# Two experts' weights in one piece per partition, loaded in two transfers instead of six

## The reference

```python
scores = sigmoid(xt @ w_router)                       # (tokens, 128)
_, idx = top_k(scores + b_router, 8)
gate = sel / sum(sel) * 2.5
for every expert e, for the tokens that chose it:
    h = silu(xb @ w_e1[e]) * (xb @ w_e3[e])           # w_e1, w_e3: (128, 1024, 256)
    out[tok] += (h @ w_e2[e]) * gate                  # w_e2: (128, 256, 1024)
y = layer_norm(alpha * h + shared_expert + out)
```

## Time and profile before

| what | value |
|---|---|
| median of three runs | 2010.45 us |
| the profiled execution: its own time | 2014.95 us |
| its span, first to last instruction | 2013.2 us |
| mean granted TensorE clock | 0.948 of full speed |
| PE busy | 1789.9 us, 89% |
| DVE, ACT, POOL busy | 630.3, 392.0, 362.4 us |
| moved by DMA | 532.04 MB, of it 488.47 MB by q1 and 41.23 MB by q0 |

### The profile page before, as it was taken

The page is one execution under the profiler, slowest core; times in us unless marked ns, Lnnn a source line. Parts: engine busy times, 40 slices in busy tenths (PEclk is TensorE's granted clock), DMA queues, the critical chain, the costliest instruction groups (busy, mean ns, idle before and its releaser), DMA issues. The chain is left out here.

```text
span 2013.2 us, 29270 instructions
## 1 busy us (share of the span) xinstructions
PE 1789.9 (89%) x10614; PEld 1055.3 (52%) x10614; DVE 630.3 (31%) x1516; ACT 392.0 (19%) x918; POOL 362.4 (18%) x529
## 2 busy tenths in 40 slices
PE   7999997889899999999988878888888888888877
PEld 6857776878778885555433333333333333333332
DVE  1387754774304412521111111111111111111127
ACT  0114544433120101311111111111111111111103
POOL 1000001888880000011111111111111111111100
PEclk8999998989999999999998999998989898989988
DMA  3433312001142425379999999999999999999966
GB/s 118 146 138 105 105 32 48 3 7 47 53 158 80 131 71 187 122 284 418 421 420 415 412 416 404 420 407 410 402 410 396 411 398 407 413 410 419 409 265 250
DMA packets 160782, 532.04 MB, mean 264 GB/s; under 512 B 22061, under 2 KB 88927, under 8 KB 110205
## 3 DMA queue, kind: packets, MB, share of 16 engines
q1 hardware_dynamic: 138921, 488.47, 61.5%
q0 software_dynamic: 20640, 41.23, 5.5%
q10 hardware_dynamic: 1148, 1.34, 0.2%
HBM read 522.52 MB, written 41.42 MB: 280 GB/s over the span
## 5 line engine op out<-in xcount | busy, mean ns | idle before, releaser
L1938 PE MATMUL bank<-arena 128*64 128x512 f32 x2048 | 511.2, 657 | 143.1 <-DMA arena<-in_w_e 141.9
L1938 PEld LDWEIGHTS bank<-arena 128*64 128x64 f32 x2048 | 158.5, 151 | 491.2 <-issue 489.7
L1956 PE MATMUL bank<-arena 128*64 128x512 f32 x1024 | 233.9, 599 | 0.0
L2181 DVE TENSOR_TENSOR arena<-bank,arena 128x256 f32<-128x256 f32 x64 | 27.2, 425 | 580.7 <-ACT arena L2026 580.7
L1806 POOL DMA_INDIRECT arena<-h_rows,index x66 | 66.9, 1013 | 774.4 <-DVE index L2055 717.9
L1425 PE MATMUL bank<-arena 128*128 128x276 f32 x768 | 184.7, 400 | 7.3 <-ACT arena L1527 3.1
L1425 PEld LDWEIGHTS bank<-arena 128*128 128x128 f32 x768 | 146.7, 192 | 41.4 <-ACT arena L1527 3.5
L1201 PE MATMUL bank<-arena 64*64 64x64 f32 (+2 forms) x2816 | 126.7, 246 | 26.7 <-DVE arena L1314 14.7
L2026 ACT ACTIVATE arena<-bank 128x256 f32<-128x256 f32 x64 | 24.6, 385 | 606.2 <-PE bank L1938 606.2
L1201 PEld LDWEIGHTS bank<-arena 64*64 64x64 f32 x2816 | 111.9, 141 | 33.4 <-DVE arena L1314 15.7
L1956 PEld LDWEIGHTS bank<-arena 128*64 128x64 f32 x1024 | 67.8, 136 | 110.8 <-issue 109.6
(11 more groups left out here) (333 smaller groups left out, 1844.0 us busy)
## 6 DMA issues: line engine op xcount, KB each, us to landing
arena<-in_w_e SPq DMA_DIRECT2D x384, 1024.0 KB, 14.2
arena<-in_w_in SPq DMA_DIRECT2D x50, 512.0 KB, 4.2
arena<-routed_rows SPq DMA_DIRECT2D x8, 2048.0 KB, 23.3
arena<-in_w_mem_kv SPq DMA_DIRECT2D x4, 1024.0 KB, 5.8
arena<-in_cache_mem_k SPq DMA_DIRECT2D x8, 512.0 KB, 4.6
arena<-in_cache_mem_v SPq DMA_DIRECT2D x8, 512.0 KB, 5.4
arena<-in_w_out SPq DMA_DIRECT2D x2, 2048.0 KB, 12.6
arena<-in_w_s SPq DMA_DIRECT2D x3, 1024.0 KB, 10.4
```

What stands on the lines that cost most here:

```text
L1938: mm = pe.matmul(p_gu[t * S:(t + 1) * S, :], xt[:, v, c, t * S:(t + 1) * S], w13[2 * v + t][:, :, c, :], start=(c == 0), stop=(c == KD - 1))
L1956: mm = pe.matmul(p_y[h][t * S:(t + 1) * S, :], hidT[:, j, t * S:(t + 1) * S], w2[2 * v + t][:, j, h * 512:(h + 1) * 512], start=(j == 0), ...
```

## The change

The host lays out the three arrays of experts as one, `w_e`, of shape (64 pairs, 128 partitions, 12288 numbers): for each pair and partition first 32 KB with the gate and up weights of both experts, then 16 KB with the down weights of both. The loads of a pair become one transfer with 32 KB per partition and one with 16 KB per partition; PE waits for 16 in each case. The buffers take the same places in SBUF and the same bytes are read from them by the same products. From one partition's piece to the next the distance in HBM is now 48 KB; it was 8 KB. Nothing else is moved: when SP issues a load, into which buffer, and what it waits for stay as they are.

```diff
-def load_w13(sp, m, io, e, buf, sem):
-    w = m.at(O_WEXP[buf], 3, 2 * D)
-    for x, name in enumerate(("w_e1", "w_e3")):
-        src = io[name][0][ds(e, 1)].rearrange("e (p c) n -> p (e c n)", c=KD)
-        sp.dma_start(w[:, x, :], src).then_inc(sem, 16)
-
-def load_w2(sp, m, io, e, buf, sem):
-    w = m.at(O_WEXP[buf], 3, 2 * D)
-    src = io["w_e2"][0][ds(e, 1)].rearrange("e (p c) n -> p (e c n)", c=2)
-    sp.dma_start(w[:, 2, :], src).then_inc(sem, 16)
+def load_w13(sp, m, io, q, buf, sem):
+    src = io["w_e"][ds(q, 1), :, 0:W13].rearrange("q p n -> p (q n)")
+    sp.dma_start(m.at(O_WPAIR[buf], W13), src).then_inc(sem, 16)
+
+def load_w2(sp, m, io, q, buf, sem):
+    src = io["w_e"][ds(q, 1), :, W13:2 * WEXP].rearrange("q p n -> p (q n)")
+    sp.dma_start(m.at(O_WPAIR[buf] + W13, 2 * WEXP - W13), src).then_inc(sem, 16)
...
-        def load(r, done, v, e):
+        def load(r, done, v, q):
             sp.wait_ge(s_gu, NP * r + done + 1)
-            for t in range(2):
-                load_w13(sp, m, io, e + t, 2 * v + t, s_w13[v])
+            load_w13(sp, m, io, q, v, s_w13[v])
             sp.wait_ge(s_y, NP * r + done + 1)
-            for t in range(2):
-                load_w2(sp, m, io, e + t, 2 * v + t, s_w2[v])
+            load_w2(sp, m, io, q, v, s_w2[v])
...
-                    pe.wait_ge(s_w13[v], (64 * NP // 2) * r + 64 * i + 64)
+                    pe.wait_ge(s_w13[v], (16 * NP // 2) * r + 16 * i + 16)
...
-                    pe.wait_ge(s_w2[v], (32 * NP // 2) * r + 32 * i + 32)
+                    pe.wait_ge(s_w2[v], (16 * NP // 2) * r + 16 * i + 16)
...
+    arrays["in_w_e"] = np.concatenate([np.stack([inputs[n].reshape(NE // 2, 2, P, 2 * D) for n in names], 3)
+                                       .transpose(0, 2, 1, 3, 4).reshape(NE // 2, P, -1)
+                                       for names in (("w_e1", "w_e3"), ("w_e2",))], 2)
```

More of the change, by code:

```diff
@@ L60 @@
 WEXP = 6 * 1024
+W13 = 8 * 1024
 O_XT = 0
@@ L1341, with prefetch_pair @@
 assert O_MERGED + KD * NT <= O_EXT
-def load_w13(sp, m, io, e, buf, sem):
-    w = m.at(O_WEXP[buf], 3, 2 * D)
-    for x, name in enumerate(("w_e1", "w_e3")):
-        src = io[name][0][ds(e, 1)].rearrange("e (p c) n -> p (e c n)", c=KD)
-        sp.dma_start(w[:, x, :], src).then_inc(sem, 16)
-def load_w2(sp, m, io, e, buf, sem):
-    w = m.at(O_WEXP[buf], 3, 2 * D)
-    src = io["w_e2"][0][ds(e, 1)].rearrange("e (p c) n -> p (e c n)", c=2)
-    sp.dma_start(w[:, 2, :], src).then_inc(sem, 16)
-def prefetch_expert(sp, m, io, e):
-    load_w13(sp, m, io, e, e, m.sem(f"expert_w13_{e // 2}"))
-    load_w2(sp, m, io, e, e, m.sem(f"expert_w2_{e // 2}"))
+def load_w13(sp, m, io, q, buf, sem):
[4 more added lines that the diff above has]
+    sp.dma_start(m.at(O_WPAIR[buf] + W13, 2 * WEXP - W13), src).then_inc(sem, 16)
+def prefetch_pair(sp, m, io, q):
+    load_w13(sp, m, io, q, q, m.sem(f"expert_w13_{q}"))
+    load_w2(sp, m, io, q, q, m.sem(f"expert_w2_{q}"))
 def merge_programs(m, io):
@@ L1649 @@
 O_SCORE = O_MSTAT + 64
-O_WEXP = (O_TOP, O_TOP + WEXP, 0, WEXP)
+O_WPAIR = (O_TOP, 0)
 AHEAD = 2
@@ L1704, in mix_programs @@
     hid, sil, hidT, gates = m.at(O_HE, DE), m.at(O_SE, DE), m.at(O_HTE, 2, P), m.at(O_GATES, 4)
-    weights = [m.at(o, 3, 2 * D) for o in O_WEXP]
-    w13 = [w[:, 0:2, :].rearrange("p x (c n) -> p x c n", c=KD) for w in weights]
-    w2 = [w[:, 2, :].rearrange("p (c n) -> p c n", c=2) for w in weights]
+    w13 = [m.at(o + 4 * D * t, 2, 2 * D).rearrange("p x (c n) -> p x c n", c=KD) for o in O_WPAIR for t in range(2)]
+    w2 = [m.at(o + W13 + 2 * D * t, 2, D) for o in O_WPAIR for t in range(2)]
     sem = m.sem
@@ L1737, in sync @@
         sp.wait_ge(sem("x_again_1"), 16)
-        for e in (2, 3):
-            prefetch_expert(sp, m, io, e)
+        prefetch_pair(sp, m, io, 1)
         for i, (c0, n) in enumerate(TILES):
@@ L1742, in sync @@
                 sp.wait_ge(s_z, NTT)
-                for e in (0, 1):
-                    prefetch_expert(sp, m, io, e)
+                prefetch_pair(sp, m, io, 0)
             sp.wait_ge(s_h, i + 1)
@@ L1763, in sync @@
                 for v in range(2):
-                    load(r, 2 * i + v, v, 4 * i + 4 + 2 * v)
+                    load(r, 2 * i + v, v, 2 * i + 2 + v)
             with sp.If(r < count - 1):
                 for v in range(2):
-                    load(r, NP - 2 + v, v, 2 * v)
+                    load(r, NP - 2 + v, v, v)
         res, w2s = m.at(O_RES, NTT, D), m.at(O_W2S, 2, D)
@@ L2399 @@
     "w_o_c": (1, W, D), "w_out": (1, D, D), "ln1_g": (1, D), "ln1_b": (1, D), "ln2_g": (1, D), "ln2_b": (1, D),
-    "w_router": (1, D, NE), "b_router": (1, NE), "w_e1": (1, NE, D, DE), "w_e3": (1, NE, D, DE),
-    "w_e2": (1, NE, DE, D), "w_s1": (1, D, DE), "w_s3": (1, D, DE), "w_s2": (1, DE, D),
+    "w_router": (1, D, NE), "b_router": (1, NE),
+    "w_s1": (1, D, DE), "w_s3": (1, D, DE), "w_s2": (1, DE, D),
 }
@@ L2412, in build @@
     io = {n: nc.dram_tensor(f"in_{n}", s, F32, kind="ExternalInput").ap() for n, s in SHAPES.items()}
+    io["w_e"] = nc.dram_tensor("in_w_e", (NE // 2, P, 2 * WEXP), F32, kind="ExternalInput").ap()
     io |= {n: nc.dram_tensor(n, s, F32, kind="ExternalOutput").ap() for n, s in OUTPUTS}
```

## The result

| | median us | runs | range |
|---|---|---|---|
| before | 2010.33 | 4 | 2005.78 to 2011.72 |
| changed | 2051.75 | 4 | 2049.09 to 2056.68 |

The changed kernel is slower: the ratio is 1.0216, with a 95% interval of 1.0194 to 1.0237, so +41 us. The forecast was slower by 7 us in a range that ended at 2045. The profiled execution of the changed kernel took 2049.09 us, its span is 2047.4 us and its mean granted clock 0.917 (0.948 before).

What follows compares the result with a forecast made beforehand. DMA bytes were taken to bound the expert loop; packet savings gave a 16.43 us step, late gathers 17.0, so 16.8 was taken: +0.12 x 62 = +7.4 us on the median, 2018 us, range 1995 to 2045.

Steps and rivals of the forecast that it cites:

- the turns: On the DMA engines, q0 and q1 alternate packet by packet, so larger weight pieces delay a gather from 8.4 to 12.9 us.
- the reading in which what is ahead of its first packet counts as bytes: Time ahead of a gather's first packet stays 2.8 us, so it lands in 12.9 us; the reading taken.
- The other reading, 17.4 us: Nine weight pieces stay ahead of each gather, landing it in 17.4 us; rival much slower, 2086 us, chance 0.07.
- The rival with the gather hidden: Gathers land in 10.1 us or less, the step is 16.43 us, the time 1995 us; chance 0.36.
- the price of the stream: In the loop's weight loads, fewer, larger packets save 0.25 us per step, -15.5 us over 62 steps.
- The cost per piece: Each weight piece costs about 7 ns, besides 303 ns per 8 KB.
- the cover: In all 62 loop steps, PE's wait for gathers mostly replaces its wait for weights, leaving +7.4 us in all.
- the size of the later step: The loop step was taken as 16.8 us against a mean of 16.68, +0.12 us for each of 62 steps.
- my upper limit for gathers alone, 17.0: With gathers alone as the limit, the step is 12.9 us landing plus 4.1 us before issue, 17.0 us.
- the clock as a reason to go high: Slow clock after PE's wait would fall on transposes and down products, before the next gather; a step near the upper limit, unpriced.
- what the gathers' queue carries: Queue q0 has 18 packets per step and engine, nine gather and nine scatter; the slower scatter was costed at nothing in the loop.

Runs made afterwards that it cites:

- e7: Changed kernel with the loop's gather replaced by a transfer of 16 rows of 64 bytes, the scatter kept; 1936.16 us, ratio 0.9631 to the kernel before.
- e8: Kernel before with the loop's gather replaced by a transfer of 16 rows of 64 bytes; 1951.96 us, ratio 0.9715 to the kernel before.
- e3: Changed kernel's layout loaded in pieces of 16 KB, gate and up in two transfers, down in one; 2000.75 us, ratio 0.9942 to the kernel before.
- e9: Two transfers per pair as in the changed kernel, but laid out for pieces of 4 KB; 2048.40 us, ratio 1.0205 to the kernel before.
- e12: Changed kernel with gate and up loads issued in the first eight steps as four transfers of 8 KB pieces; 2037.80 us, ratio 1.0126 to before.
- e11: Changed kernel with five extra, unused products of 256 columns on PE behind gate and up; 2035.90 us, ratio 1.0127 to the kernel before.
- e5: Changed kernel with PE finding slots and turning hidden rows before it waits for gathered rows; 2018.86 us, ratio 1.0059 to the kernel before.
- e1: Two transfers per pair as in the changed kernel, but laid out for pieces of 8 KB; 2007.19 us, ratio 0.9977 to the kernel before.
- e2: Changed kernel's layout, rows 48 KB apart, loaded in six transfers of 8 KB per partition; 2007.42 us, ratio 0.9979 to the kernel before.
- e4: Changed kernel with the wait for gathered rows and the transposes moved behind the down products; 2038.79 us, ratio 1.0135 to the kernel before.

## Why the prediction was wrong

**Right: the turns.** The gather was to land in 12.9 us, by the reading in which what is ahead of its first packet counts as bytes. It landed in 12.4, and in 10.6 with pieces of 16 KB. The other reading, 17.4 us, falls. The wait moved from the weights to the transposes (over 100 us of it were forecast, 129.9 came), and the steps became more even. The rival with the gather hidden is refuted by the same rows.

**Right: the price of the stream.** 15.5 us less were to come from fewer packets. e7 against e8 shows 16 (9 to 25), and the later steps of e3 show it in a kernel with gathers. The cost per piece was too low for small ones (e9: 17 ns, not 7).

**Wrong: the cover.** The step that failed is "so its wait on PE mostly takes the place of the wait for weights", applied to all 62 steps. It holds only where PE waits for weights. In the first eight steps it doesn't: PE is the limit there, with weights loaded ahead and the shared expert's products in four of them, and each late gather counts whole. That is 21 us for which the sum had nothing: some 11 of waits and as much again of products at the low clock behind them. e12, without late gathers there, has the 21 us back. I read the loop's mean step, 16.68 us, and a window that begins at 1016; the mean is made of eight steps of 15.84 and 55 of 16.81, and the window began where the first kind ends. The page had the sign: the wait for weights can't be everywhere if PE is at 9 tenths up to slice 20, some 125 us into the loop, and at 8 after it.

```profile
PE   7999997889899999999988878888888888888877
```

**Wrong: the size of the later step.** I took 16.8 us against 16.68, so +0.12. Against the right base, 16.81, the measured 17.09 is +0.28: at my upper limit for gathers alone, 17.0, and a little above. I had named the clock as a reason to go high and put no number on it. It is nearly the whole of this part: after a wait the gather is issued after 5.76 us, not 4.1, and with the clock kept up (e11) the later step is 16.83, what I had forecast for it. 55 x 0.28 = 16 us, of which e11 gives back 15.

So the sum reads 21 (first eight, PE the limit, e12) + 16 (later steps, nearly all the clock, e11) = 37 us, and not 7. Over the whole loop the low clock behind the waits is then some 26 of the 37, an estimate from 15 in the later steps and half of 21 in the first. The spans of the two profiled executions are 34 us apart, 2047.4 against 2013.2, since what lies around the loop was 2.7 us shorter in the changed one; the medians' 41 have the spread between executions in them. The end isn't later: from the last scatter on it takes 72.4 us, and took 73.7.

**Not counted: what the gathers' queue carries.** I counted nine turns for the gather and let the scatter cost nothing. The 18 turns per step stand in the earlier trace rows, and the 18 packets of the new q1 in my own text, but I didn't set the one against the other. In e5 q0 is hardly ever empty, and an early gather lands late all the same. And the DMA share of 0.99, where I expected 0.97 to 0.98, doesn't show the dry stretches; the GB/s do, 400 and not 410.

The rule of the Trainium skill ("DMA: Bandwidth & Descriptors", Queues, rings and completion order), by which an engine drains a packet of several descriptors from one queue before it switches, would have had a gather's nine pieces go together, and so land in about 10 us at most, by the prediction's estimate, and be hidden. The trace disagrees: 12.4 us, and packets of q0 and q1 that start in nearly equal numbers in each half microsecond from 1420.5 to 1424.5, where groups of nine would come in bursts. By the same page of the Trainium skill, Rules for kernel authors, small transfers are to be joined, with 1 MiB or more in each. The transfers here had 1 MB already, and going from six to two of them is worth 0.2% (e1 against the kernel before); the piece per partition, not the transfer, is what has an effect.

What stays open: why exactly the steps behind e12's change of size are slower than the changed kernel's later ones, and whether e12 and e11 together would give back all of it; that wasn't tried. Nor was the extra work of e11 put in the late steps alone, so the share of the clock in the first eight is read from step lengths and not from a run of its own.

## What to carry to other kernels

A larger piece per partition saves a few nanoseconds of packet time each, but here the other queue on the same DMA engines got one packet through per piece, so count the packets per step of every queue. Here 16 KB is the best of four sizes: about 2001 us, 0.4 to 0.6% faster than before, against 2007 for 8 KB and about 2050 for 4 and for 32 KB. Before a wait is costed as hidden, split the loop by its limits (here eight steps with loads ahead and more work on PE, then 55 without), since a mean step belongs to neither; and price the products behind a new wait at the low clock.

## What was not expected of the hardware

- Recorded packet times were longer just behind a load that found the engines dry: 1.7 us on average behind the one issued at 1434.90, against 1.22 for a piece of 32 KB. The share of 0.99 stood beside 400 GB/s and not 410, so a share near 1.00 is no proof of a full stream.
- Pieces of 4 KB cost more than the forecast from larger ones: 167 ns each in the loop and not 159, so 334 ns per 8 KB against 317 for one piece (e9).
- Rows 48 KB apart are read as quickly as rows that lie together (e2: 318 ns per 8 KB piece, 317 before).
- PE's clock fell in steps whose single waits were under 1.2 us (e4: down products 5.35 us). Five more products in place of idle time made the kernel 16 us quicker (e11).
